# Last gate chunk worked by thirds of tokens, merged rows converted in nine groups behind it

## The reference, cut to what matters

```python
u = rmsnorm(x) @ w_in            # z | xBC | dt | q,k,v of 3 groups | z_att | q_mem | z_mem | gates
y_ssd = ssd_branch(...)          # conv, chunked scan of 128 tokens, gated norm
y_att = o_att * silu(z_att)      # dilated window attention
y_mem = mem_attn(...) * silu(z_mem)
gates = sigmoid(gate_raw).reshape(b, t, 3, D_MODEL)
merged = (gates[:, :, 0] * (y_ssd @ w_br_ssd) + gates[:, :, 1] * (y_att @ w_br_att)
          + gates[:, :, 2] * (y_mem @ w_br_mem))
y = rmsnorm(x + merged @ w_out)
```

## Time and profile before

| what | value |
|---|---|
| median of 3 runs | 2118.82 us |
| profiled execution, its own time | 2122.49 us |
| its span (first to last instruction) | 2120.6 us |
| PE busy | 1978.7 us (93%) |
| DVE, ACT, POOL busy | 984.6, 763.9, 241.5 us |
| PE's share in the chain that ended last | 76% |

### The profile page before, as it was taken

The page is one execution under the profiler, slowest core; times in us unless marked ns, Lnnn a source line. Parts: engine busy times, 40 slices in busy tenths (PEclk is TensorE's granted clock), DMA queues, the critical chain, the costliest instruction groups (busy, mean ns, idle before and its releaser), DMA issues.

```text
span 2120.6 us, 34809 instructions
## 1 busy us (share of the span) xinstructions
PE 1978.7 (93%) x14301; PEld 1887.0 (89%) x14301; DVE 984.6 (46%) x1941; ACT 763.9 (36%) x1642; POOL 241.5 (11%) x358
## 2 busy tenths in 40 slices
PE   5999999999979999999999899999999859969997
PEld 5899999999979999999999898769999759969997
DVE  5313676535465353534236676103454545454423
ACT  5223354223343333323555322215566532132202
POOL 1001111100001010111111200001121111100000
PEclk9999999999999999999999999999999869989999
DMA  6211332311101111122246675683455536454422
GB/s 216 90 42 52 93 92 82 93 46 48 40 30 51 54 49 57 61 64 83 68 147 220 224 255 163 228 281 124 150 160 176 202 102 191 166 181 137 144 83 105
DMA packets 171742, 257.18 MB, mean 121 GB/s; under 512 B 20229, under 2 KB 115269, under 8 KB 171557
## 3 DMA queue, kind: packets, MB, share of 16 engines
q1 hardware_dynamic: 149328, 187.97, 28.1%
q0 software_dynamic: 22256, 66.98, 9.3%
HBM read 188.13 MB, written 66.76 MB: 120 GB/s over the span
## 4 chain that ended last, share of the span: by engine, by line
PE 76%; DVE 8%; ACT 6%; DMA 5%; issue 3%; SPq 0%; DVEq 0%; POOL 0%; ACTq 0%; POOLq 0%
PE bank L2287 19%; PE bank L2288 19%; PE bank L2289 19%; PE bank L2483 2%; DVE w_lo L1753 2%; PE bank L2698 2%; PE bank L2458 2%; DMA acc<-acc_T 2%; PE bank L2441 1%; PE bank L2587 1%; PE bank L2419 1%; ACT soft L1579 1%; PE bank L2742 1%; PE bank L2520 1%; DMA sums<-sum_T 1%
## 5 line engine op out<-in xcount | busy, mean ns | idle before, releaser
L2287 PE MATMUL bank<-w_hi,hT_hi 128*128 128x256 f32 (+1 forms) x1848 | 535.7, 290 | 1.4 <-issue 1.4
L2288 PE MATMUL bank<-w_lo,hT_hi 128*128 128x256 f32 (+1 forms) x1848 | 523.8, 283 | 0.0
L2289 PE MATMUL bank<-w_hi,hT_lo 128*128 128x256 f32 (+1 forms) x1848 | 522.9, 283 | 0.0
L2287 PE MATMUL bank<-hT_hi,w_hi 128*128 128x352 f32 x1344 | 450.8, 335 | 6.3 <-DVE acc L2134 5.6
L2289 PE MATMUL bank<-hT_hi,w_lo 128*128 128x352 f32 x1344 | 438.9, 327 | 0.0
L2288 PE MATMUL bank<-hT_lo,w_hi 128*128 128x352 f32 x1344 | 438.2, 326 | 0.0
L2287 PEld LDWEIGHTS bank<-w_hi,hT_hi 128*128 128x128 f32 (+1 forms) x1848 | 348.7, 189 | 3.2 <-issue 1.6
L2289 PEld LDWEIGHTS bank<-w_hi,hT_lo 128*128 128x128 f32 (+1 forms) x1848 | 349.6, 189 | 0.6
L2288 PEld LDWEIGHTS bank<-w_lo,hT_hi 128*128 128x128 f32 (+1 forms) x1848 | 348.7, 189 | 1.3
L2287 PEld LDWEIGHTS bank<-hT_hi,w_hi 128*128 128x128 f32 x1344 | 257.7, 192 | 20.1 <-issue 8.4
L2288 PEld LDWEIGHTS bank<-hT_lo,w_hi 128*128 128x128 f32 x1344 | 258.5, 192 | 0.5
(11 more groups left out here) (423 smaller groups left out, 2926.1 us busy)
## 6 DMA issues: line engine op xcount, KB each, us to landing
w_raw<-in_w_in SPq DMA_DIRECT2D x96, 512.0 KB, 5.0
kvring<-in_cache_win_kv SPq DMA_DIRECT2D x98, 256.0 KB, 4.7
feat_T<-fstage POOLq DMA_DIRECT2D x40, 528.0 KB, 4.0
fstage<-feat_T SPq DMA_DIRECT2D x16, 528.0 KB, 4.6
xc<-feat_T SPq DMA_DIRECT2D x8, 1024.0 KB, 5.8
sums<-sum_T SPq DMA_DIRECT2D x32, 256.0 KB, 4.5
o_rows<-obuf POOLq DMA_DIRECT2D x48, 132.0 KB, 2.0
mo<-o_rows SPq DMA_DIRECT2D x24, 264.0 KB, 3.6
```

The source lines that it names most:

```text
L2287: pe.matmul(out, xh(k), wh(k), start=(k == 0), stop=False)
L2288: pe.matmul(out, xh(k), wl(k), start=False, stop=False)
L2289: ins = pe.matmul(out, xl(k), wh(k), start=False, stop=(k == nk - 1))
```

## The change

The last gate chunk is done third by third (f0 j0, f1 j0, f0 j1, f0 j2, f1 j1, f1 j2 instead of f0 j0..2, f1 j0..2). Once both blocks of a third are through, nothing reads that third of the columns in `hT`, and rows of the merged input may be written there. So ("ya", g) is now one of nine groups: three, three or two row blocks by one third of tokens. A group waits for its third alone, and a p1 step for the groups that it reads (two or three of each third, by branch). The slots go 0, 1, 2, 0, 1, 2, 0, 1, 0. All nine are put into the list by hand (`behind`), the first ones a chunk earlier. Chunk 51's split (the weights of chunk 53) stands behind its fourth step instead of its last, and its low part right behind that. The p1 steps begin in SSD chunk 6 instead of 7 and are spread over all that is left of the SSD list; the split of a p1 chunk comes with its last step. Between ("ssd", 8, 4) and ("ssd", 8, 6) there are two more empty groups.

```diff
+YA_ROWS = (slice(0, 3), slice(3, 6), slice(6, 8))
+YA_SLOT = (0, 1, 2, 0, 1, 2, 0, 1, 0)
+N_YA = len(YA_SLOT)
...
-    core += [[("ssd", NB - 1, 5)], [("ssd", NB - 1, 6)], [("ssd_state",)], [("ssd", NB, 0)]]
+    core += [[("ssd", NB - 1, 5)], [], [("ssd", NB - 1, 6)], [("ssd_state",)], [("ssd", NB, 0)]]
...
-    core += [[("ssd_st",)], [("ssd_sy",)]]
-    core += [[("ssd", NB, q)] for q in (4, 5, 6)] + [[], []] + [[("yb", k)] for k in range(KT8)]
-    n_gate, n_ya = 31, 4
-    core[n_gate - 3] += [("yal", k) for k in range(3)]
...
+    core += [[("ssd_st",)], [("ssd_sy",)], [("ssd", NB, 4)], [("ssd", NB, 5)], [], [], [("ssd", NB, 6)], [], []]
+    core += [[("yb", k)] for k in range(KT8)]
+    n_gate = 5 * (NB - 2) + 1
+    steps = gate_steps(len(fill_src))
+    last_gate = len(chunks) - 1
+    f00, f01, f02, f10, f11, f12 = [x[:1] for x in steps[-6:]]
+    steps[-6:] = [f00, f10, f01, f02 + [("split", last_gate)], f11, f12]
+    sched += spread(core[:n_gate], steps)
...
+    behind(("feat", g, 1, 0), 0, [("ya", 0)])
+    behind(("ssd", NB - 4, 6), 0, [("ya", 1), ("yal", 3)])
+    behind(("ssd", NB - 3, 4), 0, [("ya", 2), ("yal", 4), ("yal", 5)])
+    behind(("split", g), 0, [("low", g)])
+    behind(("feat", g, 1, 1), 0, [("ya", 3), ("ya", 4)])
+    behind(("feat", g, 1, 2), 0, [("yal", 6), ("ya", 5)])
+    behind(("ssd", NB - 2, 1), 0, [("p1g", 0, 0), ("yal", 7), ("ya", 6), ("p1g", 0, 1)])
+    behind(("ssd", NB - 2, 2), 0, [("ya", 7), ("yal", 8)])
+    behind(("p1", g + 1, 0, 0, 0), 0, [("ya", 8)])
...
                 elif s[0] == "ya":
-                    k = s[1]
-                    if k == 0:
-                        act.wait_ge(s_pj, n_act_proj)
-                    act.wait_ge(s_kv[k % 3], kv_loads(k % 3) + 16 * (k // 3 + 1))
-                    act.activation(yAh[:, k, :], ya_slot(k), ACT.Copy).then_inc(s_yah, 1)
+                    g = s[1]
+                    act.wait_ge(s_pj, gates_read[g // 3])
+                    act.wait_ge(s_kv[YA_SLOT[g]], kv_loads(YA_SLOT[g]) + ya_loads(YA_SLOT[g], g + 1))
+                    act.activation(ya_part(yAh, g), ya_slot(g), ACT.Copy).then_inc(s_yah, 1)
...
-                    if s[0] == "p1" and u == n_act_proj:
-                        pe.wait_ge(s_yal, KT8)
+                    if s[0] == "p1" and u < n_act_proj + 6:
+                        pe.wait_ge(s_yal, 3 * s[4] + 2 + s[3])
```

More of the change, by code:

```diff
@@ L305, in plan, with behind @@
         core.append([("ssd", c, 4)])
-    core += [[("ssd", NB - 1, 5)], [("ssd", NB - 1, 6)], [("ssd_state",)], [("ssd", NB, 0)]]
+    core += [[("ssd", NB - 1, 5)], [], [("ssd", NB - 1, 6)], [("ssd_state",)], [("ssd", NB, 0)]]
     core += [[("ssd", NB, q)] for q in (1, 2, 3)]
     core += [[(q, b)] for b in range(BS) for q in ("ssd_sb", "ssd_sd", "ssd_so")]
-    core += [[("ssd_st",)], [("ssd_sy",)]]
-    core += [[("ssd", NB, q)] for q in (4, 5, 6)] + [[], []] + [[("yb", k)] for k in range(KT8)]
-    n_gate, n_ya = 31, 4
-    core[n_gate - 3] += [("yal", k) for k in range(3)]
[L313 to L318, removed]
+    core += [[("ssd_st",)], [("ssd_sy",)], [("ssd", NB, 4)], [("ssd", NB, 5)], [], [], [("ssd", NB, 6)], [], []]
[6 more added lines that the diff above has]
+    sched += spread(core[:n_gate], steps)
+    def behind(step, groups, items):
+        i = sched.index(step) + 1
+        for _ in range(groups):
+            while sched[i][0] != "ssd":
+                i += 1
+            i += 1
+        sched[i:i] = items
     steps = []
@@ L328, in plan @@
                         steps[-1].append(("p1g", ft + br, 1 - br))
-        steps.append([("split", n)])
-    sched += spread(core[n_gate + n_ya:], steps)
+        steps[-1].append(("split", n))
+    sched += spread(core[n_gate:], steps)
+    g = last_gate
+    behind(("ssd", NB - 4, 4), 0, [("yal", k) for k in range(3)])
+    behind(("feat", g, 1, 0), 0, [("ya", 0)])
[7 more added lines that the diff above has]
+    behind(("p1", g + 1, 0, 0, 0), 0, [("ya", 8)])
     for i in range(4):
@@ L966, in snew, with ya_slot, ya_part, ya_loads @@
             return (Lflat[:, D:2 * D] if b % 2 == 0 else yo[:, :]).rearrange("p (i n) -> p i n", i=8)
-        def ya_slot(k):
-            return (yraw, acc1, acc0)[k % 3][:, :]
+        def ya_slot(g):
+            rows = YA_ROWS[g % 3]
+            return (yraw, acc1, acc0)[YA_SLOT[g]][:, 0:THIRD * (rows.stop - rows.start)].rearrange("p (k n) -> p k n", n=THIRD)
+        def ya_part(buf, g):
+            j = g // 3
+            return buf[:, YA_ROWS[g % 3], THIRD * j:THIRD * j + THIRD]
+        def ya_loads(at, g):
+            return 16 * sum(YA_SLOT[x] == at for x in range(g))
+        def ya_last(at, g):
+            return 1 + max(x for x in range(g) if YA_SLOT[x] == at)
+        gates_read = [1 + max(u for x, u in proj.items() if x[0] == "feat" and x[3] == j) for j in range(3)]
         def acc_of(ft):
@@ L1156, in _ @@
                 elif s[0] == "yal":
-                    k = s[1]
-                    if k == 0:
+                    g = s[1]
+                    j, rows = g // 3, YA_ROWS[g % 3]
+                    if g == 0:
                         late_free(sp)
[L1160 to L1166, removed]
+                    if g >= 3:
+                        sp.wait_ge(s_yal, ya_last(YA_SLOT[g], g))
+                    sp.dma_start(ya_slot(g), yT[8 + rows.start:8 + rows.stop, :, THIRD * j:THIRD * j + THIRD].rearrange("k p n -> p k n")).then_inc(s_kv[YA_SLOT[g]], 16)
                 elif s[0] == "p1g":
                     _, ft, br = s
-                    if br:
+                    if ft == 0:
+                        gates_stored(sp)
+                    elif br:
                         sp.wait_ge(s_p1, ft)
@@ L1662, in _ @@
                     at = k % 3
-                    act.wait_ge(s_kv[at], kv_loads(at) + 16 * len(range(at, KT8, 3)) + 16 * (k // 3 + 1))
+                    act.wait_ge(s_kv[at], kv_loads(at) + ya_loads(at, N_YA) + 16 * (k // 3 + 1))
                     if k == 6:
@@ L2110, in _ @@
                 elif s[0] == "ya":
-                    k = s[1]
-                    dve.wait_ge(s_yah, k + 1)
-                    dve.tensor_tensor(yAl[:, k, :], ya_slot(k), yAh[:, k, :].bitcast(F32), ALU.subtract).then_inc(s_yal, 1)
+                    g = s[1]
+                    dve.wait_ge(s_yah, g + 1)
+                    dve.tensor_tensor(ya_part(yAl, g), ya_slot(g), ya_part(yAh, g).bitcast(F32), ALU.subtract).then_inc(s_yal, 1)
                 elif s[0] == "yb":
                     k = s[1]
-                    dve.wait_ge(s_yah, KT8 + k + 1)
+                    dve.wait_ge(s_yah, N_YA + k + 1)
                     dve.tensor_tensor(yBl[:, k, :], yb_slot(k), yBh[:, k, :].bitcast(F32), ALU.subtract).then_inc(s_yal, 1)
```

11 lines of the change are left out of this document (5 added, 6 removed).

## The result

The changed kernel is slower: 2135.76 us (median of 4 runs, 2132.6 to 2138.03) against 2119.69 us before, ratio 1.0061, 95% interval 1.0044 to 1.0078. A second set of runs gave 1.0049 (1.0034 to 1.0065). The quotient of the two medians above is 1.0076, that of the second set 1.0045; the ratios with their intervals are the ones argued from. The forecast was 2115.6 us, 3.2 less than before, with a range from 2106 to 2123.

A forecast was written before the change was run, and what follows sets the result against it. PE, busy 93% of the span, bounds the kernel; some 42 us of waits and low clock were at stake. 2.65 us won by chunk 7 plus 0.5 at the end made 3.2 less: 2115.6 us, range 2106 to 2123.

The forecast's parts named there:

- Step 1: Early conversion groups 0 and 1: they push DVE's state work of SSD chunk 5 by 1 us, costing nothing.
- Step 2: Weight copy of chunk 53 ahead of SSD chunk 6: `yy` ends at 1688.5, PE transposes it 12 us later.
- Step 3: Conversion groups ahead of chunk 6's `Lm`: L2698 starts at 1699.1, 10.3 us later than before.
- Step 4: From chunk 6 to chunk 7: L2662 at about 1722.0 instead of 1719.34, three p1 steps done, before none.
- Step 5: SSD chunk 7: transposes at 1754.0 instead of 1752.15, nine p1 steps done instead of six; sum 2.65 us won.
- The term of 2.65 us: Sum up to chunk 7: three p1 steps ahead 5.8, less 1.85 later start, less 1.3 wait for `yst`.
- Step 6: Samples and end: the 2.65 us stay, 0 to +3 among the sample chunks, 0.5 us won at the end.
- The signs that the prediction named: Profile after: named waits and `xtok` behind `w_hi` if right; chunk 7's first L2690 over 5 us later if slower.
- the walk: The step-by-step forecast from chunk 6 to the end: 2115.6 us, its own range 2111 to 2120; chance 0.55.
- the slower one: SSD chain held by conversions, weights and group 6 landing late: 4.9 us lost, 2123.7; chance 0.16.
- the 33 us of wait and 9 of clock: PE's waits around SSD chunks 6 and 7, 33.7 us, and about 9 us lost at half clock there.

The follow-up runs named there:

- experiment 6: Changed kernel with the weight copies of chunk 53 moved behind the front half of SSD chunk 6 and chunk 5's row norm; ratio 1.0026.
- experiment 11: Changed kernel with unused matmuls in two PE waits: 56 ahead of the first p1 step, 28 ahead of chunk 6's `Lm` products; ratio 1.0036.
- experiment 3: Changed kernel with the weight copies of chunk 54 put back behind the first sample step; ratio 1.0057, and 1.0037 the second time.
- Experiment 5: Changed kernel with one p1 step moved from ahead of chunk 7's second half to between it and the state's transposes; ratio 1.0080, 2138.75 us.

## Why the prediction was wrong

Times of the forecast are put to the later start of the first trace after (3.8 us).

*Step 1* held: no cost, the later start is chance.

*Step 2* held in its mechanism: `w_hi` starts at 1684.15 where 1683.3 was forecast, `xtok` directly behind it, L2753 at 1694.24 instead of 1692.3. One of the missing 2 us is a product of DVE beside POOL (see the last section). It was priced as 12 us on the chain and, in the sum, as something that three early p1 steps outweigh; experiment 6 shows that without it about half of the loss is gone.

*Step 3* held: L2735 at 1703.37, forecast 1702.9; L2743 ended 1.6 later than forecast.

*Step 4* held within 1.6 us: L2727 at 1722.03 (forecast 1720.8), L2699 of chunk 7 at 1727.43 (1725.8).

*Step 5* failed in part. Three p1 steps were done there, as forecast, and nine by the transposes of chunk 7, but PE reached these at 1762.92 instead of 1757.8. Of these 5.1 us 1.6 were there at L2699. I took L2698 and L2706 of chunk 7 at full clock, as before (3.79 and 1.95 us); they ran 5.15 and 3.73, 3.1 more, and one p1 step behind them 3.5. The p1 steps among the waits did not bring the clock back for good. It was full until 1686.9 and again from 1697.2 to 1700.5 and from 1717.7 to 1721.0, and half between these and behind them, now while PE had work. The Trainium skill (TensorE: Matmul & The Clock Gate, Part 1) says that the throttled state is the default and that activity releases it. The trace agrees with the release: the clock was back at 1697.2, after PE had gone to work again at 1694.24 with L2753 and L2727; and experiment 11 agrees, where unused matmuls kept L2746 at 3.79 us. The term of 2.65 us was 3.95 won up to the transposes (5.8 - 1.85), less the wait of 1.3 for `yst` behind them. Of the 3.95 only 0.1 was won, on the mean of two traces; the wait came as forecast (1.27).

*Step 6* is the step that failed most. It took the time behind chunk 7 for "0 to +3" because "PE is full up to 1862" and DVE and ACT "can follow", and the end for 0.5 won. Measured: 5.5 us lost up to the samples' `Lm` products, 0.7 more to their transposes, 1.8 to p2, 8.0 in all, or 6.7 without the wait of 1.3 that step 5 had counted. PE was full there because the lists fitted, and the diff had moved the copy of chunk 54 between the decays, which I had not followed in ACT's list. It is only partly the cause: experiment 3 got 2.8 us back at that place and at most 2 in the time. What is left of the 5.5 stands in PE's other waits there: the 1.27 of L2759 for `yst`, and 1.87 (1.36 in the second trace) of L2715 for the first decay, which ACT began behind the store of the state. Experiment 5 did not remove that store's wait, and no run shows what a list without it would win. The 0.7 and the 1.8 stay open too; the wait of the samples' L2753 shrank by 2.9 (5.54 for 8.41) where 3.9 was forecast.

The signs that the prediction named came out as it said they would if it was right: `xtok` directly behind `w_hi`, the waits of 11.91, 5.77 and 1.27 us, three p1 steps ahead of L2699, 5.54 us ahead of the samples' L2753. The first L2727 of chunk 7 (1736.88) was 1.1 us behind the walk, where over 5 was to mean slower. None of the signs looked at the clock of chunk 7 or at the samples' decays, where the forecast failed.

Of the rivals, the slower one came closest in time (2123.7), for another reason: it needed late loads (L2735 later than 1702.5 in the times of before, it was at 1699.6). That of the 33 us of wait and 9 of clock "most is therefore still there" (step 4) was right and was the argument for no gain; I still let three steps of p1 work count as won, and that rested on the least certain of the steps.

## What to carry to other kernels

When conversions and a serial chain share in-order engines, put the chain's instructions first in every list and look in each list (the DMA issuer's too) for an instruction that waits ahead of them; here that was worth 0.4 to 0.9% against the kernel before, and giving PE earlier work, with it or instead of it, won nothing that these runs can show. Moving filler work into a wait shortens the run only if the chain behind the wait does not move; compare the chain's own points, with the work done by then, and not the waits. And follow a copy that "comes with" a moved step through every engine's list, up to the next serial stretch.
